# Hymba layer with hierarchical MoE on one core: the first eight attention steps re-dealt (last projection units, SSM gate, order of the output product's rows)

## The reference, cut to what matters

```
h = rms_norm(x, ln1_g)                       # x: 1024 x 1024
proj = h @ w_in                              # 1024 -> 2304 columns
q1,q2,k1,k2,v,conv_in,ssm_in = split(proj)   # 4 heads, q/k 64 wide, v 128 wide
p = softmax(q1 k1 * s + bias) - lam * softmax(q2 k2 * s + bias)    # causal
a = rms_norm(p @ v, subln_g) * (1 - lam_init)                      # 512 columns
c = silu(layer_norm(depthwise_conv31(glu(conv_in))))               # 256 columns
g = gelu(ssm(ssm_in))                                              # 256 columns
s = g * sigmoid(g @ glu_w + glu_b)
x = x + concat([a, c, s]) @ w_out
h2 = rms_norm(x, ln2_g)
x = x + moe(h2)        # top-1 of 4 groups, top-2 of its 8 experts, 32 experts
out = rms_norm(x, final_g)
```

## Time and profile before

| | us |
|---|---|
| median of three runs | 1231.2 |
| lowest and highest | 1229.65, 1232.02 |
| the profiled execution, its own time | 1231.33 |
| its span in the trace | 1229.6 |
| TensorE busy in the span | 1142.1 |

### The profile page before, as it was taken

The page is one execution under the profiler, slowest core; times in us unless marked ns, Lnnn a source line. Parts: engine busy times, 40 slices in busy tenths (PEclk is TensorE's granted clock), DMA queues, the critical chain, the costliest instruction groups (busy, mean ns, idle before and its releaser), DMA issues.

```text
span 1229.6 us, 16168 instructions
## 1 busy us (share of the span) xinstructions
PE 1142.1 (93%) x5022; PEld 547.6 (45%) x5023; DVE 466.2 (38%) x1011; ACT 366.2 (30%) x736; POOL 287.9 (23%) x227
## 2 busy tenths in 40 slices
PE   6999999998899999994899999987999999999990
PEld 5897444454346666654233333322333333333330
DVE  3550039942446666446222323312232332322313
ACT  3221100025455556412223232222322223323223
POOL 0110299920000000101022122222212212122123
PEclk9999999999899999997799999989999999999995
DMA  8127111012411111177692999999799999999217
GB/s 254 26 39 140 35 35 35 0 69 74 171 35 59 63 50 37 52 296 298 231 375 31 359 374 375 410 414 413 284 364 378 396 404 378 404 361 409 99 21 276
DMA packets 86157, 261.95 MB, mean 213 GB/s; under 512 B 31927, under 2 KB 49086, under 8 KB 61518
## 3 DMA queue, kind: packets, MB, share of 16 engines
q1 hardware_dynamic: 68868, 243.43, 51.6%
q0 software_dynamic: 11520, 16.81, 6.2%
q10 hardware_dynamic: 5706, 0.92, 0.4%
HBM read 244.86 MB, written 26.74 MB: 221 GB/s over the span
## 4 chain that ended last, share of the span: by engine, by line
PE 88%; DMA 5%; ACT 2%; DVE 2%; issue 1%; POOL 0%; SPq 0%; DVEq 0%; ACTq 0%; POOLq 0%
PE psum L1349 28%; PE psum L1368 14%; PE psum L1058 13%; PE psum L1248 9%; PE psum L1055 4%; PE psum L1202 3%; DMA W<-in_w_gate 3%; PE psum L1335 3%; PE psum L1222 3%; PE psum L1053 2%; PE psum L1356 2%; PE psum L1213 2%; PE psum L1277 1%; DMA W<-in_x 1%; PE psum L1266 1%
## 5 line engine op out<-in xcount | busy, mean ns | idle before, releaser
L1349 PE MATMUL psum<-W,RD 128*64 (+1 forms) x800 | 371.9, 609 | 15.4 <-DVE RD L1869 14.5
L1350 PE MATMUL psum<-W,RD 128*64 128x512 f32 x800 | 371.9, 609 | 0.0
L1349 PEld LDWEIGHTS psum<-W,RD 128*64 128x64 f32 x800 | 107.4, 140 | 229.0 <-issue 223.1
L1368 PE MATMUL psum<-W,RD 128*64 (+1 forms) x400 | 184.0, 603 | 2.3 <-ACT RD L981 2.3
L709 POOL DMA_INDIRECT x_rows<-RD,tabi x49 | 79.7, 1627 | 452.2 <-ACT RD L988 442.5
L1369 PE MATMUL psum<-RD 128*64 128x512 f32 x400 | 184.0, 603 | 0.0
L1851 DVE TENSOR_TENSOR RD<-psum,RD 128x256 f32<-128x256 f32 x50 | 21.3, 425 | 420.6 <-ACT RD L977 420.6
L1058 PE MATMUL psum<-W 128*128 128x512 f32 x384 | 166.4, 593 | 0.6 <-ACT W L794 0.6
L1248 PE MATMUL psum<-W,RD 128*128 128x512 f32 x256 | 119.9, 602 | 1.6 <-ACT RD L870 1.1
L1058 PEld LDWEIGHTS psum<-W 128*128 128x128 f32 x384 | 72.5, 190 | 89.7 <-issue 88.7
L1350 PEld LDWEIGHTS psum<-W,RD 128*64 128x64 f32 x800 | 107.4, 140 | 0.0
(11 more groups left out here) (324 smaller groups left out, 1269.3 us busy)
## 6 DMA issues: line engine op xcount, KB each, us to landing
W<-in_w_up SPq DMA_DIRECT2D x32, 2048.0 KB, 13.3
W<-in_w_gate SPq DMA_DIRECT2D x32, 2048.0 KB, 18.2
W<-in_w_down SPq DMA_DIRECT2D x32, 2048.0 KB, 20.1
W<-in_x SPq DMA_DIRECT2D x16, 512.0 KB, 4.7
W<-in_w_in SPq DMA_DIRECT2D x5, 1024.0 KB, 11.6
W<-in_w_in SPq DMA_DIRECT2D x16, 256.0 KB, 4.3
x_rows<-W SPq DMA_DIRECT2D x8, 512.0 KB, 2.9
h_rows<-RD SPq DMA_DIRECT2D x8, 512.0 KB, 3.6
```

Source lines behind the costliest of these rows:

```text
L1349: pe.matmul(bank(2)[0:HALF].rearrange("p (g n) -> p g n", g=2), x, near, start=k == 0, stop=k == KD - 1)
L1350: ins = pe.matmul(bank(2)[HALF:P], x, upgate1[:, k].rearrange("p g n -> p (g n)"), start=k == 0, stop=k == KD - 1)
L1368: pe.matmul(out[0:HALF], a, W[:, bass.ds(base + (2 * KD * FF + D * k), 512)], start=k == 0, stop=k == FK - 1)
```

## The change

The two late units are dealt over steps 0 to 6 in parts of 3, 2, 2, 1 and 3, 3, 2 matmuls by a table, and the copy of the first one moves from step 1 to step 3, that of the second from step 3 to step 6. The four gate parts go one to a step, 0 to 3. VectorE's gate work is cut in halves of 1024 columns, in steps 2 and 4, and stands behind `combine` instead of ahead of it. The output product takes the rows in the order 6, 7, 4, 5, 0, 1, 2, 3, and its waits are spread: part 0 of step 8 waits for the last unit's copy, rows 6 and 7 of `w_out` and both gate halves, part 1 for rows 4 and 5 and the convolution, step 9 for rows 0 to 3.

```diff
+FILLS = {0: (0, 0, 3), 1: (0, 3, 2), 2: (0, 5, 2), 3: (0, 7, 1), 4: (1, 0, 3), 5: (1, 3, 3), 6: (1, 6, 2)}
+PROJ_ORDER = (6, 7, 4, 5, 0, 1, 2, 3)
...
@@ ScalarE, loop over k
-                if k < 2:
-                    misc(12 + 2 * k)
-                    misc(13 + 2 * k)
-                if k in (1, 3):
-                    evac(EARLY_UNITS + k // 2)
+                if k < 4:
+                    misc(12 + k)
+                if k in (3, 6):
+                    evac(EARLY_UNITS + k // 6)
...
@@ TensorE, fill(k, part)
-                if k < 4:
-                    unit(EARLY_UNITS + k // 2, 4 * (k % 2) + 2 * part, 2)
+                if k in FILLS:
+                    u, k0, n = FILLS[k]
+                    near = n - n // 2
+                    if part == 0:
+                        unit(EARLY_UNITS + u, k0, near)
+                    elif n > near:
+                        unit(EARLY_UNITS + u, k0 + near, n - near)
                 elif 8 <= k < 8 + 4 * NT:
                     i, step = (k - 8) // 4, (k - 8) % 4
                     half, own = step // 2, step % 2 == 1
                     if k == 8 and part == 0:
-                        for s in range(3):
-                            pe.wait_ge(wout_in[s], 16)
+                        pe.wait_ge(unit_ev, len(UNITS))
+                        pe.wait_ge(wout_in[2], 16)
+                        pe.wait_ge(ssm_ok, 2)
+                    if k == 8 and part == 1:
+                        pe.wait_ge(wout_in[1], 16)
                         pe.wait_ge(conv_ok, 4)
-                        pe.wait_ge(ssm_ok, 1)
+                    if k == 9 and part == 0:
+                        pe.wait_ge(wout_in[0], 16)
...
-                        c = (0 if own else 4) + 2 * part + q
+                        c = PROJ_ORDER[(4 if own else 0) + 2 * part + q]
                         ins = pe.matmul(bank(proj_bank(j)), mixT[:, c, i * P:(i + 1) * P], wout[:, c, 512 * half:512 * half + 512],
-                                        start=c == 4, stop=c == 3)
+                                        start=c == PROJ_ORDER[0], stop=c == PROJ_ORDER[-1])
...
@@ VectorE, loop over k
-                if k == 3:
-                    dve.wait_ge(misc_ev, FIRST_HEAD)
-                    gl = RG[:, 2048:4096]
-                    link(dve.tensor_scalar(gl, gl, 0.5, 0.5, ALU.mult, ALU.add))
-                    dve.tensor_tensor(RD[:, 6144:8192], RG[:, 4096:6144], gl, ALU.mult).then_inc(ssm_ok, 1)
-                    dve.wait_ge(ssm_ok, 1)
...
                 if 1 <= k <= NI:
                     combine(k - 1)
+                if k in (2, 4):
+                    c = k // 2 - 1
+                    dve.wait_ge(misc_ev, FIRST_HEAD - 2 + 2 * c)
+                    gl = RG[:, 2048 + 1024 * c:3072 + 1024 * c]
+                    link(dve.tensor_scalar(gl, gl, 0.5, 0.5, ALU.mult, ALU.add))
+                    dve.tensor_tensor(RD[:, 6144 + 1024 * c:7168 + 1024 * c], RG[:, 4096 + 1024 * c:5120 + 1024 * c], gl, ALU.mult).then_inc(ssm_ok, 1)
+                    dve.wait_ge(ssm_ok, c + 1)
```

## The result

| | before | after |
|---|---|---|
| median, us | 1230.76 (4 runs) | 1219.74 (4 runs) |
| lowest and highest | 1229.65, 1232.02 | 1219.33, 1220.61 |
| the profiled execution, its own time | 1231.33 | 1219.34 |
| its span | 1229.6 | 1217.6 |
| mean granted clock of the span | 0.966 | 0.973 |

The ratio is 0.9911, 95% interval 0.9899 to 0.9924: the change makes the kernel faster by 11.0 us. The forecast was 1222.6 in a range of 1219.5 to 1227.5. The time lies at the low edge of that range, 0.2 us inside it. Two later comparisons of the same two kernels gave 0.9922 [0.9909, 0.9936] and 0.9920 [0.9899, 0.9941]: 9.6 and 9.8 us by the ratio, 10.4 us both times by the medians. By the mean of all runs of this study the kernel before stands at 1229.9 (58 runs) and the changed kernel at 1219.9 (16 runs), a gain of 9.9 us.

What follows compares the result with a forecast made beforehand. TensorE carries 88% of the chain, so only its idle time and slow clock pay: 3.2 us of idle plus 5.5 us of clock make 8.7, from 1231.33 to 1222.6 us, range 1219.5 to 1227.5.

Steps and rivals of the forecast that it cites:

- The gain reaches the end: Expert weight issues move along with TensorE, so 8.7 us arrive; rival of the gain lost downstream, about 1230.5 us, chance 0.09.
- The clock: Of 13.6 us at half clock, 11.0 are work taking 5.5 at full clock; 5.5 us come back.
- The rival with a fall of the clock: The clock falls all the same around steps 7 and 8 or step 0: 1224.3 to 1226 us, chance 0.36.
- The idle time: TensorE's waits between 295 and 345 us shrink from 6.6 to 3.4 us, a gain of 3.2.
- Step 0: TensorE idles 1.5 us from 301.3 to about 302.8, as scores 1 wait for the exponentials of step 0.
- step 4: The second unit's first matmul waits for the first unit's copy in the shared bank 7: 0.5 us.
- Step 7: No filler, and ScalarE has the second unit's copy ahead: 2.8 us for the step, 1.4 of them idle.
- The steps between: Steps 1 to 6 are bound by TensorE's own work; waits for gate parts and exponentials go there.
- the check by the steps: Step 8 begins 6.0 us earlier, step 9 at 334.5 instead of 343.08 us, which is 8.6.
- The gate's cover: VectorE's gate halves in steps 2 and 4 cost zero under covers of 2 us and 1 us.
- The order of the rows: Output product in steps 8 and 9: the new row order itself costs or brings nothing.
- The late rows: Rows 4 and 5 of w_out land late and step 8 waits: 1233 to 1236.5 us, chance 0.07.

Runs made afterwards that it cites:

- a4: The kernel before with one more unused matmul of 512 columns in each of steps 4 to 7; 1226.67 us, ratio 0.9971.
- c1: The changed kernel with the old row order and all waits ahead of step 8's first product, repeated on another chip; 1222.37 us.
- a1: The changed kernel with the gate whole at step 3 ahead of the combine and the old row order and waits; 1228.98 us.
- a2: The changed kernel with the gate in one piece behind the combine of step 4; 1220.4 us.
- a3: The kernel before with only the new row order of the output product and its spread waits; 1229.73 us, ratio 1.0001.

## Why the prediction was right, and where not

**The gain reaches the end.** Forecast 8.7 us, measured 9.6 between step 0 and step 9 in three traces, and 9.9 over all runs. Both terms erred to the same side, 0.8 us in the idle time and 0.1 in the clock, and the range held by only 0.2 us in the first comparison (0.4 by the mean of all runs). The issues of expert weights move along as said: the two of the earlier trace rows, at 531.00 and 558.58 us before, stand at 521.64 and 549.22.

**The clock.** Forecast 5.5 us. The changed kernel's 9.6 less the 4.0 of idle are 5.6; a4 gives 5.0 with the idle cut for another reason. This term stands, and so does where it comes from: steps 4 to 7, in which TensorE had neither filler nor more than short work between its idles. Whether the missing wide matmuls or the idles count isn't separated: both the change and a4 alter the two together. The rival with a fall of the clock didn't show in three traces. It is real for a kernel beside this one: c1 has it, after idles of 0.6 and 1.1 us.

**The idle time.** Forecast 3.4 us left, measured 2.6. Step 0 kept 1.41 (forecast 1.5) and step 4 0.37 (0.5). Step 7 is the term that was mis-sized: 2.8 us with 1.4 of work and 1.4 idle were forecast, 2.52 with 1.75 of work and 0.77 idle came, so that two misses partly cancel in its length. The prediction put the second unit's copy in full between the scores and the exponentials. ScalarE's timeline has it beside scores 7, which begin at 325.64:

```profile
325.52 0.60 ACT L798 ACTIVATE W<-psum 128x512 f32<-128x512 f32 x1 [0.35 <-PE psum L1061]
```

**The steps between** went as walked: no gate waits, no waits for exponentials in steps 1 to 6. Counted from step 0, step 9 came 1.0 us sooner than the walk had it. Of that, 0.3 are step 7 and 0.6 are steps 1 to 3, where the prediction didn't add up: from 302.8, its own prices (4.0, 4.2 and 3.5 us for these steps) lead to 314.5, and it wrote 315.1. Measured are 4.05, 4.12 and 3.49 us, from 303.02 to 314.68. The forecast rests on idle and clock and isn't touched by this slip; the check by the steps is, and without it gives 9.2 us instead of 8.6, nearer to the 9.6 measured than the sum's 8.7.

**The gate's cover.** The two covers, forecast as 2 us and 1 us, show as VectorE's idle ahead of the next statistics, 1.12 and 1.07 us:

```profile
309.48 1.23 DVE L1732 TENSOR_TENSOR RD<-W 128x1024 f32<-128x1024 f32 x1
311.83 0.29 DVE L1619 CUSTOM_DVE_ANT_0 W<-psum,band 128x128 f32<-128x128 f32 x1 [1.12 <-PE psum L1205]
...
317.56 1.23 DVE L1732 TENSOR_TENSOR RD<-W 128x1024 f32<-128x1024 f32 x1
319.85 0.42 DVE L1619 CUSTOM_DVE_ANT_0 xr<-psum,band 128x256 f32<-128x256 f32 x1 [1.07 <-PE psum L1205]
```

The first half ended at 310.7 and not by 309.5, since it begins behind the combine of its step (308.76) and not when its tanh is done. Cost zero was right. What the prediction did not see is how much hangs on the move behind the combine: a1, without it and without the new order of the rows, has nothing of the gain in its runs, and 6.3 of the 7.5 us that its trace loses stand at the gate. The halves add nothing (a2).

**The order of the rows.** "The order of the rows itself costs or brings nothing" was wrong. It is true of the kernel before (a3). In the changed kernel the transfer of rows 4 and 5 is issued 2.5 us later and lands at 330.4, while step 8 now wants its first rows at 329.3. The prediction had a landing of 330.6, a need at 331.7 and a product that starts 1.7 us before that; it used them for the margin and didn't ask what the margin would be in the old order: below zero. So the old order would have cost 2.8 of the 9.9 us by the runs. A wait of 1.1 us, 1.4 us at step 9, is seen in both traces; a fall of the clock behind it costs 1.6 more where it comes, in one of three traces with the old order. How often it falls, and whether the expert loop's second block has a part in the rest, stays open.

**The late rows** didn't come, but the margin was thinner than forecast: part 1 of step 8 begins at 331.0 instead of 331.7, 0.6 us behind the landing instead of 1.1. Their price is now measured: 12.6 us at a landing of 15.6 us, where 10.3 to 14.0 were worked out for 14.5. Slower than the kernel before, as that rival said.

## What to carry to other kernels

When filler is dealt out anew, ask of each piece what it stood in front of. Here VectorE waited in order for a gate part that came later, and a weight transfer tied to the last filler came 2.5 us later; the first could take most of the gain, the second part of it, and each needed an edit of its own. Fill the steps that have no wide matmul first: even unused work paid there. Compare a kernel with itself in several traces before a gain of 1 or 2 us is laid to an edit.

## What was not expected of the hardware

Whether the clock falls behind the same idle differs between executions of one kernel: with the same kernel, the expert loop's second block ran at the full clock in one trace and partly at half in two, 11.98 against 13.66 and 14.50 us, and all fourteen traces of the study show one of these three lengths within 0.1 us. And a short transfer's place in its queue set its landing: 1 MB took 4.9 us ahead of 4 MB of weights and 15.6 us behind them.
